# Block products taken kind by kind, token sums spread over sixteen units, weight sums issued at other units, in a one-core decoder layer

## The reference, cut to what matters

```python
h = rmsnorm(x, g_mix_pre); z = h @ w_in
y_a = mla_branch(q_lat, c_kv, k_pe, ...) @ w_attn_br
y_p = pool_branch(u_pool, ...) @ w_pool_br
merged = sigmoid(gate_a) * y_a + sigmoid(gate_p) * y_p
x = x + rmsnorm(merged @ w_mix_out, g_mix_post)
...
kv = (mem_n @ w_mem_kv).reshape(B, N_MEM, 2, MEM_HEADS, MEM_HEAD_DIM)
k, v = kv[:, :, 0], kv[:, :, 1]
...
h = rmsnorm(x, g_ffn_pre)
a = h @ w_ffn_in                  # 2048 -> 11264, then a causal convolution of width 3
x = x + rmsnorm((gelu(gate) * up) @ w_ffn_out, g_ffn_post)   # 5632 -> 2048
```

## Time and profile before

| | |
|---|---|
| median of 3 runs | 1772.9 us (1772.37 to 1773.26) |
| the profiled execution's own time | 1771.83 us |
| its span, first to last instruction | 1770.1 us |
| PE busy | 1753.1 us, 99% |
| DVE busy | 1202.3 us, 68% |
| ACT busy | 953.8 us, 54% |
| POOL busy | 138.9 us, 8% |
| DMA packets | 411.65 MB, mean 233 GB/s |

### The profile page before, as it was taken

One profiled execution on the slowest core, in us unless ns is written; L12 is line 12 of the kernel. 1 busy time (PEld: TensorE's weight loads), 2 busy tenths in 40 slices (PEclk: granted clock), 3 DMA queues, 4 the chain that ended last, 5 costly groups with the idle time before them and its releaser, 6 DMA issues.

```text
span 1770.1 us, 25239 instructions
## 1 busy us (share of the span) xinstructions
PE 1753.1 (99%) x8906; PEld 1476.7 (83%) x8906; DVE 1202.3 (68%) x1685; ACT 953.8 (54%) x1295; POOL 138.9 (8%) x212
## 2 busy tenths in 40 slices
PE   9999999999999999999999999999999999989998
PEld 7888888888888788878888888888888888878886
DVE  6555555655456887676665487777777777886666
ACT  7555555565446665554554474444444444455554
POOL 4000111011000110000000101111111000000002
PEclk9999999999999999999999999999999999999999
DMA  8478698998866675686445569999999965578785
GB/s 297 148 235 222 175 264 209 283 211 268 231 229 247 210 251 183 214 270 235 149 143 190 187 231 291 275 279 285 270 284 272 266 196 184 195 231 278 236 278 201
DMA packets 227208, 411.65 MB, mean 233 GB/s; under 512 B 19734, under 2 KB 46278, under 8 KB 225734
## 3 DMA queue, kind: packets, MB, share of 16 engines
q1 hardware_dynamic: 202742, 340.51, 57.9%
q0 software_dynamic: 22848, 58.73, 17.0%
q10 hardware_dynamic: 1552, 11.54, 1.7%
HBM read 406.55 MB, written 62.91 MB: 265 GB/s over the span
## 4 chain that ended last, share of the span: by engine, by line
PE 93%; DVE 4%; DMA 1%; ACT 1%; issue 0%; SPq 0%; DVEq 0%; ACTq 0%
PE bank L1306 18%; PE bank L705 11%; PE bank L707 10%; PE bank L706 10%; PE bank L1308 9%; PE bank L1037 6%; PE bank L1039 6%; PE bank L1038 6%; PE bank L1133 3%; PE bank L1232 3%; DVE wlo L2022 2%; PE bank L1233 2%; PE bank L1134 2%; PE bank L919 1%; PE bank L730 1%; DMA raw<-in_w_in 1%
## 5 line engine op out<-in xcount | busy, mean ns | idle before, releaser
L2022 DVE TENSOR_TENSOR wlo<-raw,whi 128x1024 fp32r<-128x1024 f32 (+1 forms) x646 | 793.9, 1232 | 499.5 <-ACT whi L1469 284.0
L1469 ACT ACTIVATE whi<-raw 128x1024 fp32r<-128x1024 f32 x312 | 330.2, 1060 | 374.4 <-PE bank L1308 209.6
L1306 PE MATMUL bank<-actA,whi 128*128 128x512 f32 x1344 | 472.1, 394 | 0.0
L1308 PE MATMUL bank<-actA,wlo 128*128 128x256 f32 x1344 | 380.2, 283 | 0.0
L1306 PEld LDWEIGHTS bank<-actA,whi 128*128 128x128 f32 x1344 | 252.4, 188 | 58.3
L1431 ACT ACTIVATE whi<-raw 128x1024 fp32r<-128x1024 f32 x174 | 184.0, 1060 | 151.0 <-PE bank L1039 142.1
L1308 PEld LDWEIGHTS bank<-actA,wlo 128*128 128x128 f32 x1344 | 252.7, 188 | 0.0
L1455 ACT ACTIVATE whi<-raw 128x1024 fp32r<-128x1024 f32 (+1 forms) x159 | 166.5, 1050 | 133.4 <-PE bank L707 55.6
L705 PE MATMUL bank<-whi,actA 128*128 128x512 f32 x460 | 187.7, 408 | 1.2 <-ACT v_sb L1481 1.2
L707 PE MATMUL bank<-whi,actA 128*128 128x512 f32 x460 | 181.5, 395 | 0.0
L706 PE MATMUL bank<-wlo,actA 128*128 128x512 f32 x460 | 181.5, 395 | 0.0
(11 more groups left out here) (372 smaller groups left out, 2579.1 us busy)
## 6 DMA issues: line engine op xcount, KB each, us to landing
raw<-in_w_ffn_in SPq DMA_DIRECT2D x88, 1024.0 KB
raw<-in_w_in SPq DMA_DIRECT2D x46, 1024.0 KB
raw<-in_w_ffn_out SPq DMA_DIRECT2D x76, 512.0 KB, 5.2
raw<-weight_sums SPq DMA_DIRECT2D x56, 512.0 KB, 5.2
raw<-in_w_attn_br SPq DMA_DIRECT2D x16, 1024.0 KB
raw<-in_w_mem_kv SPq DMA_DIRECT2D x16, 1024.0 KB
raw<-in_w_mem_q SPq DMA_DIRECT2D x16, 1024.0 KB
raw<-in_w_mem_o SPq DMA_DIRECT2D x16, 1024.0 KB
```

What stands on the lines that cost most here:

```text
L1306: pe.matmul(dst[:, :], whi[:, s, o:o + P], actA[:, :, kt, :], start=(kt == 0), stop=False)
L1308: mm = pe.matmul(dst[:, 0:S], wlo[:, s, o:o + P], actA[:, 0, kt, :], start=False, stop=(kt == KD - 1))
L1469: act.activation(whi[:, ks % AHEAD, 0:w], raw[:, c, ks % 2, 0:w], ACT.Copy).then_inc(hi_done, 1)
L2022: dve.tensor_tensor(wlo[:, vs % AHEAD, 0:w], raw[:, c, vs % 2, 0:w], f32(whi[:, vs % AHEAD, 0:w]), ALU.subtract).then_inc(lo_done, 1)
```

## The change

`pair_units` takes the form units kind by kind (all groups of `w11`, then all of `w21`, and so on) instead of group by group; this holds for `MIXED`, `VALUES`, `PAIR0` and `PAIR1`. The strings of `PAIR0` and `VALUES` change as well: the first changes where form and plain units alternate, the second has its last form unit one place earlier. The token sums of `FOUT` stand in every second round from 9 to 23, their rounding in rounds 12, 16, 20 and 24, their subtraction in rounds 14, 18, 22 and 26. The weight sums' steps 0 to 3 wait for `V_YP` + 0, 4, 8, 12 units (before: steps 0 and 1 for + 0 and 8), steps 4 + 2i and 5 + 2i for units 6 and 11 of quad i (before: steps 2 + 3i to 4 + 3i for units 18, 26 and 34), steps 12 and 13 for `V_YA` + 2 and 8.

```diff
     def pair_units(p, groups, kinds, ku=KF // 2):
 
-        forms = iter([(p, g, f) for g in range(groups) for f in FORMS])
+        forms = iter([(p, g, f) for f in FORMS for g in range(groups)])
         plain = iter([(p, k, c) for c in range(2) for k in range(2 * groups, ku)])
         return [next(forms if kind == "F" else plain) for kind in kinds]
 
     EACH = "FsFFsFsFFsF"
-    PAIR0 = pair_units(0, GF, "s" * 9 + EACH * GF + "s" * 3)
+    PAIR0 = pair_units(0, GF, "s" * 9 + "FsFFsFFsFsFFsFsFFsFs" + "FFs" * 8 + "sss")
     PAIR1 = pair_units(1, GF, "F" + "s" * 4 + EACH[1:] + EACH * (GF - 1) + "s" * 8)
-    VALUES = sum((pair_units(p, GV, "F" + "sFF" * 4 + "sFFF" + "sFF" + "ss", KD // 2) for p in range(2)), [])
+    VALUES = sum((pair_units(p, GV, "F" + "sFF" * 4 + "sFFF" + "FF" + "sss", KD // 2) for p in range(2)), [])
...
+    XS_AT, XS_HIGH_AT, XS_LOW_AT = tuple(range(9, 25, 2)), (12, 16, 20, 24), (14, 18, 22, 26)
...
-        weight_sum_steps(V_YP, 0, 2, 0, EARLY_SUMS, 8)
+        weight_sum_steps(V_YP, 0, 4, 0, EARLY_SUMS, 4)
         for i in range(ND):
+            weight_sum_steps(V_ATT + 24 * i + 6, 4 + 2 * i, 6 + 2 * i, 0, EARLY_SUMS, 5)
             for t in range(TT):
                 pool.wait_ge(acc_out[t], U_ATT + 4 * i + 3)
                 ya = bufY[:, t, i * NC:(i + 1) * NC]
                 pool.tensor_tensor(ya, ya, gp_sb[:, t, :], ALU.mult).then_inc(mp_ok, 1)
-            weight_sum_steps(V_ATT + 24 * i + 18, 2 + 3 * i, 5 + 3 * i, 0, EARLY_SUMS, 8)
+        weight_sum_steps(V_YA + 2, 12, 2 * EARLY_SUMS + 2, 0, EARLY_SUMS, 6)
...
-            if n in (7, 10, 12, 14):
-                xs_split((7, 10, 12, 14).index(n))
+            if n in XS_HIGH_AT:
+                xs_split(XS_HIGH_AT.index(n))
...
-            if n == 2:
-                dve.wait_ge(w_used, V_FOUT)
-            if n in (2, 6, 8, 9, 10, 11, 12, 13):
-                token_sums(gT, XF, GF, (2, 6, 8, 9, 10, 11, 12, 13).index(n), xs_step, xs_full)
-            if n in (9, 11, 13, 15):
-                i = (9, 11, 13, 15).index(n)
-                sum_low(XS[TOKEN_SUMS[i]], XF[TOKEN_SUMS[i]], i, xs_hi, xs_lo)
+            if n in XS_AT:
+                token_sums(gT, XF, GF, XS_AT.index(n), xs_step, xs_full)
+            if n in XS_LOW_AT:
+                f = TOKEN_SUMS[XS_LOW_AT.index(n)]
+                sum_low(XS[f], XF[f], XS_LOW_AT.index(n), xs_hi, xs_lo)
```

## The result

The changed kernel takes **1777.27 us** (median of 10 runs, 1772.69 to 1780.27), the kernel before 1772.94 beside it (10 runs, 1771.71 to 1776.86). The ratio is 1.0021, with a 95% interval of 1.0011 to 1.0031: slower by 0.2%, where 1768.1 and faster was predicted. Its profiled execution took 1776.44 us, 4.6 more than that of before, and its span is 1774.7. So the loss differs from run to run; what follows is the account of the profiled one.

A forecast was written before the change was run, and what follows sets the result against it. PE, busy 99% of the span, bounds the kernel, so only its waits count. FOUT -3.9, VALUES -0.6 and branch stage -0.3 sum to -4.8 us: 1767.0 against the profiled 1771.83, 1768.1 on the median's scale; range 1765.8 to 1771.6.

The forecast's parts named there:

- FOUT: Token sums stage: the xs wait and clock fall (6.4 us) go, 2.5 us of wlo waits come; -3.9 us.
- VALUES: Second pair's second unit: PE's wait for memv, 0.6 us with start-up, goes; -0.6 us.
- Quads 1 and 3: Branch stage: PE's v_sb waits go since even steps start after units 8 to 11's loads; -1.5 us.
- Quad 0: Branch stage: units 10 and 11's load lands late beside step 3, a v_sb wait like quad 1's; +1.2 us.
- SP waits for no step here: Branch stage: said that SP, which issues the loads, is not held by the weight sums' steps; no size given.
- The upper bound: Quad 0: about 5 us lost if units 8 and 9 are late as well, and the next loads behind them.
- the first rival: Quad 0: loads keep near half of each engine beside a step, no new wait; total -6.0, 1766.9 us; chance 0.19.
- The rival of a longer wait: Quad 0: wait of 3 to 5 us where small rows and three steps meet; 1770 to 1772 us; chance 0.11.
- The rival on the slower side: Loads fall behind over all of quad 0, PE loses about 8 us and 1.6 for the clock; 1776.5; chance 0.07.

The follow-up runs named there:

- d4: e3 with the token sums of FOUT back in the rounds of the kernel before; 1768.48 us, 0.9981 of before.
- f2: e3 with the old strings of PAIR0 and VALUES; 1767.59 us, 0.9973 of before.
- e4: e3 with the token sums of FOUT begun earlier, in rounds 2 to 23; 1762.96 us, 0.9950 of before.
- d1: Changed kernel without weight sums' steps in quad 0; steps 0 to 3 stay, 4 to 9 in quads 1 to 3, last four in V_YA; 1772.99 us, 1.0006 of before.
- e3: Changed kernel with only steps 0 and 1 in V_YP, two steps mid-quad in each quad, last four in V_YA; 1766.40 us, 0.9970 of before.
- d3: e4 with one step more beside the head units' loads (step 2 at V_ATT unit 0), last three in V_YA; 1762.76 us, 0.9951 of before.
- d2: Changed kernel with the accumulating transfers of steps 1 to 5 made plain, same size and places; 1766.73 us, 0.9974 of before.
- f1: Changed kernel with the head units' loads reading long rows (2048 or 1024 bytes), from wrong columns; 1765.56 us, 0.9962 of before.
- e2: Kernel before with only the changed places of the weight sums' steps; 1781.67 us, 1.0053 of before.

## Why the prediction was wrong

**FOUT: right.** Predicted a wait of 2.1 us for `wlo` near 1577 and 0.4 two units on, without a fall of the clock. Measured, with the start-up, 1.9 and 0.26, clock 1.00. The first begins at 1587.3, some 10 us late, which is what quad 0 cost beyond the plan. The count of DVE's passes also gave the sizes of d4 (4.7 against 4.3), f2 (3.3 against 3.0) and e4 (none, and none was there).

**VALUES: right**, -0.6; f2 puts the wait back.

**Quads 1 and 3: right**, -1.5, no wait is left.

**Quad 0: wrong, +10.8 where +1.2 was predicted.** The steps' times were right. The step that failed is: "The load of units 10 and 11 of quad 0 goes out at 164.60, in the middle of step 3, just as in quad 1. With 15 us it lands at 179.6 to 180.4". The duration was near (16.7), but the issue came 8.4 us later, since SP was still held in issuing the load before; it landed at 189.7. "SP waits for no step here" was true of semaphores alone. That accounts for the second wait, which d1 shows to need step 4 beside the load as well. The larger loss, the first wait, has no term in the sum at all: the loads of units 4 to 7 were left out of it. Unit 4's already held ACT for 1.52 us, and unit 6's, issued up to 171.61, was used from 178.94. The upper bound, "about 5 us", had the wrong units in it as well.

Three things made the loss together, since each one taken away takes all or nearly all of it: a second step right behind the first beside these loads (e3 and d3), the accumulation (d2) and the short rows (f1). Each step made the loads fall short, and in the kernel before there had always been time to catch up. In quad 1 step 2 ended at about 226 and step 3 went out at 232.60; in the changed kernel step 3 followed step 2 within a microsecond. So q1 moved 3.67 MB from 142 to 177 us, where it had moved 7.3 MB from 144.5 to 180 before.

Behind the missing term stands a reading of one number. The earlier trace rows give 2.53 MB in step 3's 20.4 us, and the working took that as the rate beside any step. It is a mean over very unlike stretches. The DMA view of before, 238 to 243 us and 248 to 253:

```profile
q0 software_dynamic: 350, 0.68, 108.4%
...
q1 hardware_dynamic: 547, 1.10, 66.1%
q0 software_dynamic: 122, 0.22, 33.9%
```

In the first of them q1 has no row: it moved nothing, though a load of 1 MB in rows of 2 KB had been issued at 238.72. (A share over 100% says that these shares are rough.) So beside an odd step, which only accumulates, long rows can stand still too. The waits of quads 1 and 3 in the kernel before came beside odd steps, 3 and 9; the step that ran beside the same units in quad 2 without a wait, the first rival's argument, was step 6, an even one. What the short rows add is that the loads are already behind when the odd step begins (f1).

The rival of a longer wait named the place and the rows, "where small rows of `w_q_b` and `w_kv_b` and three steps meet", and gave it 3 to 5 us; measured were 10.8. The rival on the slower side had the backlog: "steps 2 to 5 each leave 1 MB undone", about 8 us and a fall of the clock, 1776.5; the median is 1777.27. Its argument against itself ("in quad 1 three steps followed each other closely and only 1.2 us were lost") does not hold: of those three only step 2 ran while head units' loads were issued, and a pause of nearly 7 us followed it. It was given 0.07. That its time came out is in part luck, since its details were not right. By its own need of 1.05 MB per 5.6 us, 3.0 and 3.6 MB were wanted beside steps 2 and 3, and 1.53 and 2.14 were moved: 1.5 MB short each, not 1. Step 4 left nothing undone (3.88 moved), and the loss came at units 6 and 10, not near 20.

The first rival had the loads keep near half of each engine. As a mean of a step the engines' time after comes near that: 39% and 41% in the first two stretches, 56% in the third. Inside step 3 it does not hold: from 164 to 171 us q1 had 16.5%, and 27.9% in f1. It also counted the half as half of the bytes, and a byte in short rows is dearer: 39.0% of 16 x 16 us for 1.53 MB is 65 us of an engine per MB, 56.3% of 16 x 19 us for 3.88 MB is 44. f1 took 1765.6, near the rival's 1766.9, but with 36.5% in its first stretch, so that agreement does not show the rule.

The Trainium skill's rule beside it (DMA: Bandwidth & Descriptors, Queues, rings and completion order) is that each engine goes round its queues packet by packet. The page means by a packet a group of descriptors. So the packets that the profile counts, 4086 of q1 beside 816 of q0, need not be the page's, and no run here tests the rule itself.

Left open: whether SP's held issue costs anything by itself. In d1 the load of units 10 and 11 was issued just as late, without a wait of PE, and the hold may be only the sign of the backlog; loads of `w_in` on another queue were not tried. Open too is why the accumulating step lets so little through at its heart.

## What to carry to other kernels

Price a transfer that runs beside others by both kinds: the row length of the loads, and whether the other transfers accumulate. Look up the bytes that the queue moved in short stretches of a few us, and do not use a mean over a whole step. When background transfers are moved, check every load in the stretch they move to, from the first, and ask whether the pause in which the loads used to catch up is still there. Follow SP's issue instructions too: where one takes more than its usual time, as here 10.24 us in place of 0.37, all later issue times move with it. A wait removed in one stage by spreading work (here the 4.2 us of FOUT) is safe when it is counted pass by pass on the engine that does it.

## What the runs showed of the hardware

- A load's issue instruction on SP can last 10.24 us in place of 0.37, with no semaphore named, when loads in short rows are queued before it and a step runs beside them; with long rows none in quad 0 took over 1.00 (f1).
- Beside three accumulating transfers of 512 KB a load of 1 MB in rows of 2 KB moved nothing from its issue at 238.72 until 243 us (kernel before).
- An accumulating DRAM to DRAM transfer holds a DMA engine about 218 ns for a packet of 1.9 KB, a plain one 216 ns for 3.6 KB (d2), both beside loads.
- TensorE's clock fell to 0.50 behind idle times of 2.85 and 4.85 us and stayed at 1.00 behind 1.74. Before the second PE had worked for only 7 us since the first. Waits of 1.1 us (e2, at 171) and 1.4 (d2) had no such stretch behind them either.
